# Reordering the chunk loop of a bidirectional state-space scan across four engines

## The reference, cut to what matters

```python
xbc = silu(depthwise_conv(xbc, w_ssm_conv[l], b_ssm_conv[l]))      # 7 taps
y_f = ssd_scan(xp, pad_front(dt_f), A[0], Bp, Cp)
y_b = fl(ssd_scan(fl(xp), fl(pad_front(dt_b)), A[1], fl(Bp), fl(Cp)))
y = (y_f + y_b)[:, PAD:] + d_skip.astype(f32)[:, None] * xf
# in ssd_scan, for each chunk of 128 tokens:
decay = exp(where(mask, seg, -inf)); cb = einsum('bclgn,bcsgn->bcgls', Cc, Bc)
y_diag = einsum('bcgls,bcgjls,bcsgjp->bclgjp', cb, decay, xd)
y_off = einsum('bclgn,bcgjpn,bcgjl->bclgjp', Cc, prev, exp(a_cs))
y = rms_norm(y * silu(z), w_ssm_norm[l]); branch_ssm = y @ w_ssm_out[l]
merged = sigmoid(gate_1) * branch_conf + sigmoid(gate_2) * branch_ssm
```

## Time and profile before

| | |
|---|---|
| device time, median of 3 runs | 2569.19 us (2568.33 to 2570.97) |
| the profiled execution, time | 2569.12 us |
| its span | 2567.1 us |
| busy: TensorE, weight load, VectorE, ScalarE, GpSimd | 95%, 60%, 63%, 32%, 16% |
| mean granted TensorE clock | 0.978 |
| DMA | 676.31 MB, mean 263 GB/s |
| chain that ended last, by engine | TensorE 69%, DMA 18%, VectorE 6%, ScalarE 4% |

### The profile page before, as it was taken

How to read it: one execution, slowest core, us unless ns; L and a number is a source line. 1 busy time by engine, 2 the same in 40 slices (tenths; PEclk the granted TensorE clock), 3 DMA queues, 4 the chain that set the end, 5 groups by cost and what they waited for, 6 DMA issues and landing times.

```text
span 2567.1 us, 41027 instructions
## 1 busy us (share of the span) xinstructions
PE 2439.5 (95%) x17615; PEld 1542.9 (60%) x17615; DVE 1610.1 (63%) x1749; ACT 821.3 (32%) x1361; POOL 406.9 (16%) x423
## 2 busy tenths in 40 slices
PE   8998899999989999999979989999999999999996
PEld 6764468888879898989879973333323233232232
DVE  4346556665539898988484641766666666666664
ACT  3256544444344645454454421000000000000001
POOL 0034011111102212123330400100000000011110
PEclk9999999999989999999989989999999999999998
DMA  5200268887745454546622467999999999999996
GB/s 201 84 33 25 94 236 288 291 285 270 269 151 187 153 188 152 193 147 210 175 100 104 182 249 304 376 411 413 411 412 412 412 412 414 413 413 411 411 413 235
DMA packets 129717, 676.31 MB, mean 263 GB/s; under 512 B 19300, under 2 KB 52068, under 8 KB 100228
## 3 DMA queue, kind: packets, MB, share of 16 engines
q1 hardware_dynamic: 56624, 554.81, 54.4%
q0 software_dynamic: 25632, 88.49, 10.2%
q10 hardware_dynamic: 47284, 30.42, 4.4%
HBM read 618.55 MB, written 55.12 MB: 262 GB/s over the span
## 4 chain that ended last, share of the span: by engine, by line
PE 69%; DMA 18%; DVE 6%; ACT 4%; issue 2%; POOL 1%; ACTq 0%; POOLq 0%; DVEq 0%
PE PS L1157 24%; DMA expert_ring_high<-w_experts 12%; PE PS L843 12%; PE PS L789 5%; PE PS L785 5%; PE PS L786 5%; PE PS L1025 4%; PE PS L1030 2%; DMA ring<-ssd_sums 2%; ACT ring L1566 2%; DMA projection_low_parts<-PREL 1%; PE PS L689 1%; PE PS L640 1%; PE PS L636 1%; PE PS L637 1%
## 5 line engine op out<-in xcount | busy, mean ns | idle before, releaser
L1157 PE MATMUL PS<-expert_ring_high,U 128*32 128x512 f32 x4240 | 472.4, 596 | 17.9 <-DMA expert_ring_high<-w_experts 17.2
L1157 PE MATMUL PS<-expert_ring_low,U 128*32 128x512 f32 x4016 | 446.9, 593 | 10.9 <-DMA expert_ring_low<-w_experts 9.3
L843 PE MATMUL PS<-XH,RINGF 128*128 128x264 f32 x2304 | 393.3, 289 | 1.2 <-ACT arena L1510 1.2
L1157 PEld LDWEIGHTS PS<-expert_ring_high,U 128*32 128x32 f32 x4240 | 136.5, 110 | 328.8 <-issue 303.0
L843 PEld LDWEIGHTS PS<-XH,RINGF 128*128 128x128 f32 x2304 | 325.3, 190 | 9.2 <-issue 6.8
L1157 PEld LDWEIGHTS PS<-expert_ring_low,U 128*32 128x32 f32 x4016 | 128.9, 110 | 309.1 <-issue 288.6
L2355 DVE SCALAR_TENSOR_TENSOR arena<-expert_ring_low,U,arena 128x2048 f32<-128x2048 f32 x134 | 305.7, 2347 | 0.0
L843 PE MATMUL PS<-UH,RINGF 128*128 128x264 f32 x1152 | 234.2, 286 | 0.0
L2088 DVE SCALAR_TENSOR_TENSOR H<-arena,par,H 128x528 f32<-128x528 f32 x240 | 187.5, 827 | 1.3
L843 PEld LDWEIGHTS PS<-UH,RINGF 128*128 128x128 f32 x1152 | 180.1, 190 | 0.0
L2355 DVE SCALAR_TENSOR_TENSOR arena<-expert_ring_high,U,arena 128x2048 f32<-128x2048 f32 x76 | 174.0, 2348 | 0.5
(11 more groups left out here) (358 smaller groups left out, 3886.3 us busy)
## 6 DMA issues: line engine op xcount, KB each, us to landing
expert_ring_low<-w_experts SPq DMA_DIRECT2D x96, 2048.0 KB, 27.7
expert_ring_high<-w_experts SPq DMA_DIRECT2D x96, 2048.0 KB, 30.3
arena<-w_proj POOLq DMA_DIRECT2D x72, 512.0 KB, 5.4
projection_low_parts<-PREL POOLq DMA_DIRECT2D x72, 512.0 KB, 4.2
ring<-w_proj SPq DMA_DIRECT2D x72, 512.0 KB, 3.6
RINGF<-projection_low_parts SPq DMA_DIRECT2D x72, 512.0 KB, 4.6
ring<-w_gu SPq DMA_DIRECT2D x11, 2048.0 KB, 10.4
ring<-ssd_sums ACTq DMA_DIRECT2D x32, 512.0 KB, 8.6
```

Source lines behind the costliest of these rows:

```text
L843: last = nc.tensor.matmul(PS[:, banks[i], 0:HT], w[:, k, :], x[:, k, lo:hi], start=start, stop=stop)
L1157: mm = nc.tensor.matmul(PS[QUAD * t:QUAD * t + QUAD, bank, :], stat(t), move(t), start=start, stop=stop)
```

## The change

It touches four lists. On GpSimd the masks move one step: the list is `XD(c)`, `XW(c)`, `masked(c + 1)` from chunk 1 on, where it was `masked(c + 2)` from chunk 0 on. On VectorE bank 6 is given back by the first read of `of`, ahead of the wait for `XD`, and the second `chunk_taps` moves behind that. On TensorE the last backward product of the last group comes between the two gate tiles of its first chunk. On ScalarE the exponentials of the last group's chunk 4 follow those of chunk 3. Behind the scan VectorE does `y_low(0)` and `y_low(1)`, the last `gate_y`, then `y_low` 2 to 7, two weight splits, `y_low` 8 to 15 and two weight splits; and GpSimd waits for four weight splits ahead of its last three `add_ln`.

```diff
--- before.py
+++ after.py
@@ -965,9 +965,15 @@
                     if c == 0:
                         open_(("cb", g, 0), 4)
                         fill(nc.tensor.matmul(PS[0:n, 4, 0:n], BF[:, 0:n], CF[:, 0:n], start=True, stop=True), ("cb", g, 0))
-                    gates((g, c))
-                    if c == 0:
+                    if c == 0 and g == GROUPS - 1:
+                        first, second = [GATE_OF[n] for n, place in enumerate(GATES_AT) if place == (g, 0)]
+                        proj(first)
                         back_state(g, 3)
+                        proj(second)
+                    else:
+                        gates((g, c))
+                        if c == 0:
+                            back_state(g, 3)
                     if c < 4 and g < GROUPS - 1:
                         conf(2 * g + CONF_AHEAD + c // 2, c % 2)
                     elif g < GROUPS - 1:
@@ -1645,8 +1651,10 @@
                 decays(g, 0)
                 decays(g, 1)
                 for c, (t0, n) in enumerate(CHUNKS):
-                    if c >= 2:
+                    if c >= 2 and not (g == GROUPS - 1 and c == NC - 1):
                         decays(g, c)
+                    if g == GROUPS - 1 and c == NC - 2:
+                        decays(g, c + 1)
                     if g == GROUPS - 1 and c + 2 < NC:
                         fr_load(g, c + 2)
                     gates_out((g, c))
@@ -2175,19 +2183,20 @@
 
                     if c > 0:
                         gate_y(g, c - 1)
-                    chunk_taps(g, c)
-                    dve.wait_ge(S("xd_ready"), i + 1)
                     yc = YC[0:n, :]
                     yh = yc.rearrange("p (h w) -> p h w", h=GH)
                     if c > 0:
                         got(dve, ("of", g, c))
-                        link(V_.tensor_tensor(yh, PS[0:n, 6, :].rearrange("p (h w) -> p h w", h=GH),
-                                              bc(EF[0:n, c, h8], n, HD), MUL))
-                        free(V_.tensor_tensor(yc, yc, XD[0:n, :], ADD), ("of", g, c))
+                        free(V_.tensor_tensor(yh, PS[0:n, 6, :].rearrange("p (h w) -> p h w", h=GH),
+                                              bc(EF[0:n, c, h8], n, HD), MUL), ("of", g, c))
                         dve.wait_ge(*freed(("of", g, c)))
+                        dve.wait_ge(S("xd_ready"), i + 1)
+                        link(V_.tensor_tensor(yc, yc, XD[0:n, :], ADD))
                         base = yc
                     else:
+                        dve.wait_ge(S("xd_ready"), i + 1)
                         base = XD[0:n, :]
+                    chunk_taps(g, c)
                     if c < 4:
                         got(dve, ("ob", g, c))
                         tmp = YB[0:n, :]
@@ -2213,18 +2222,17 @@
                             ins = V_.tensor_tensor(st, st, PS[:, 6, :], ADD)
                         free(ins, ("sf", g, c))
                         dve.wait_ge(*freed(("sf", g, c)))
-                    if g == GROUPS - 1 and c == NC - 1:
-                        for k in range(DT):
-                            y_low(k)
+            y_low(0)
+            y_low(1)
             gate_y(GROUPS - 1, NC - 1)
+            for k in range(2, DT):
+                y_low(k)
             tail_split_low(0)
             tail_split_low(1)
-            for k in range(8, 3 * QB):
+            for k in range(DT, 16):
                 y_low(k)
             tail_split_low(2)
             tail_split_low(3)
-            for k in range(3 * QB, 16):
-                y_low(k)
             conf_taps((tap[0] + DT * CONF_TAPS) // 2)
             tail_split_low(4)
             tail_split_low(5)
@@ -2560,8 +2568,8 @@
                         else:
                             got(pool, ("sb", g, 1))
                         scaled(XW[:, c % 2, :], g, c, n, W2[0:n, c, h8], "xwf_ready")
-                    if c + 2 < NC:
-                        masked(g, c + 2)
+                    if 1 <= c and c + 1 < NC:
+                        masked(g, c + 1)
                     if g == GROUPS - 1:
                         if c < 3:
                             add_ln(c + 1)
@@ -2570,6 +2578,7 @@
                                 add_y(k)
             for k in range(3 * QB, 16):
                 add_y(k)
+            pool.wait_ge(S("weights_low"), TAIL_LOW + 4)
             for u in range(4, DT - 1):
                 add_ln(u)
             pool.wait_ge(S("roots"), 4)
```

## The result

The changed kernel takes 2542.86 us (median of 5 runs, 2540.54 to 2545.98); the kernel before, run beside it, 2570.97 (2568.33 to 2572.76). The ratio is 0.9889, 95% interval 0.9878 to 0.9900: 28.1 us faster. The forecast was 2538.6 us, 30.5 less than before, with a range of 2530 to 2555.

What follows compares the result with a forecast made beforehand. TensorE was taken to bound the kernel, with its idle and slow time inside the scan winnable: 11.0 us in groups 0 to 2 plus 19.5 in the last group and first output tiles, 30.5 off 2569.12, gave 2538.6 us; range 2530 to 2555.

Steps and rivals of the forecast that it cites:

- Groups 0 to 2: First three scan groups: GpSimd's products fit inside the broadcast wait; idle 7.16 plus clock 5.1 us, 12.3 at most, 11.0 taken.
- First chunk: Last group: with the backward product between its two tiles, TensorE goes on without a wait, some 6 us earlier.
- Third chunk: Last group: with masks after the sums, its exponentials last from 1259 to 1264, below tiles until 1272.5; TensorE waits for nothing.
- Fifth chunk: Last group: exponentials follow the fourth chunk's, wait for GpSimd's mask until about 1282, end at 1285.5; chunk ends at 1295.4.
- Output tiles: Behind the last group: first tile ends at 1303.9, three more at 1321.4 against 1341.78; the 3.61 us wait goes.
- VectorE's gating comes third instead of ninth: Before the output tiles: squares and high parts of the last four rows start 17 us earlier.
- The added wait: GpSimd holds its last three convolution sums for four weight splits; VectorE gains, no engine misses the sums.
- Half: Rival: last group gives half, sums slow VectorE and one set of exponentials stays on the path; 2548.5 us, chance 0.13.
- nothing: Rival: the scan ends earlier but the tail waits for its weights or VectorE's taps; 2569 us, chance 0.05.
- A whole block: Rival: eight VectorE splits each held by a whole GpSimd sum of 1.66 us, losing 9.0 us more; 2544.6 us, chance 0.06.
- Slower: Rival: GpSimd's masks become late behind the products, 25 to 42 us if missed everywhere; 2584 us, chance 0.03.
- The signs I had named: Wrong if GpSimd's products wait for VectorE before a landed broadcast, or ScalarE waits over 3 us before fifth-chunk exponentials.

## Why the prediction was right

The waits it named are the ones that went, and 28.1 us came of 30.5. In two places luck helped, the clock of groups 0 to 2 and the first output tile. Step by step:

- **Groups 0 to 2: 11.0 forecast, 9.7 measured.** The products run inside the broadcast's wait, and VectorE never waits for exponentials there, so no mask is late where it counts (in group 0 3.64 and 1.36 us of cover are left; I had put some 3 before the fourth chunk's). The clock came back whole and gave 5.8 us, where I had 5.1 from rounded clocks: 0.7 us by luck. The term that was mis-sized is the short waits that stay: I left 1.3 us of the 12.3, and 3.31 us of the idle 7.16 stayed. Nearly all of it is L996 waiting 0.3 to 0.9 us for the output gate (3.3 us in G, before 0.4), because that gate, behind its pair of taps, has become what TensorE needs last. With that pair moved too, G fell by 2.0 us. I had also put VectorE's read of the second chunk at 865 before and 863 after; the rows have its end at 863.60 and 861.24. The step that "it need not wait here in later chunks either" held: L1002 waits nowhere for L2194.
- **Early return and mask order as two terms.** I gave them one sum, and rightly: undone alone they cost 5.3 and 11.3 us, together 9.0.
- **First chunk: 6 us forecast, 6.0 measured** with the backward product put back behind both tiles. It starts at 1222.46; I had put it near 1222.
- **Third chunk.** Its exponentials start 46.5 us into the group, forecast 1259 - 1212.3 = 46.7. The run with the old mask order confirms the chain that I named, mask, sum, square, exponentials.
- **Fifth chunk.** Its exponentials end at 75.2 us into the group; I had 73.2. They wait 1.97 us for GpSimd's fifth mask, which ends 71.9 us into the group where I had about 70. VectorE doesn't wait for these exponentials, but what stands behind them comes later by as much. That is a link that I hadn't written down: GpSimd's last `XD` product stands behind sums 9 to 11, which wait for squares that now stand behind these exponentials. The step was "fifth with 3.7 us of its own and three waits of some 0.9 us for VectorE": the three waits are 0.70, 0.29 and 3.09 us. And I had counted only VectorE's first split, not ScalarE's first weight tile, which comes last, by 0.97 us. The first output tile starts 85.3 us into the group; I had 1295.4 - 1212.3 = 83.1. These 2.2 us are nearly all of the 2.5 between the 20.4 that I worked out for L and the 17.9 measured; of the 2.5 I had allowed for 0.9 when I took 19.5.
- **Output tiles.** From the first matmul to the norm sum 26.1 us, forecast 1321.4 - 1295.4 = 26.0, and that is luck: I let the first tile wait for splits, while in fact it waits for none and runs most of its first 32 matmuls at half the clock, 6.83 us for 3.89, after TensorE's waits. The 3.61 us wait is gone, as said, and 2.50 us of it come back when the order is undone. "VectorE's gating comes third instead of ninth" gained nothing.
- **The added wait.** I called it harmless, and "VectorE gains" stands: 1.4 us of L. Beside sums a low part takes up to 1.6 to 1.8 us instead of 0.75, more than the 1217 ns average of the earlier trace rows, which was a mean of both kinds. I had also set that length against 689 ns from one start to the next; like against like, the eight lost 9.3 - 5.5 = 3.8 us and not 4.2. Four sums beside eight low parts cost 8.99 - 5.51 = 3.5 us, forecast some 3, and it is covered: no tile waits.
- **Rivals.** *Half* and *nothing* fell with L's 17.9 us and the unchanged rest. *A whole block* is nearer to what the traces show than I had allowed, only smaller. A sum takes 1.12 us where VectorE is idle (1281.80 in the changed kernel), not 1.66, and only four sums run beside the eight low parts, so the most that whole blocks could cost is 4 x 1.12 = 4.5 us, of which 3.5 were lost. It stayed under the tiles. The rule of the Trainium skill (SBUF — State Buffer, section "Who interferes with whom") is that the two engines' instructions shut each other out of a port that they share. The traces nearly agree: one low part and one sum take 1.57 us together, where a full block would make it 0.69 + 1.12 = 1.81. *Slower* was close in one place: the fourth chunk's mask in group 0 had 1.36 us to spare where I counted on some 3, and in group 1 nothing to speak of.
- **The signs I had named.** One sign of being wrong came up and cost nothing in G: in each of groups 0 to 2 GpSimd's products wait for VectorE with the landed broadcast of the fifth chunk behind them. In the last group the fifth mask, late behind sums and products, cost ScalarE 1.97 us. "No wait above 1 us before the output tiles" failed (3.09 us), the three groups gave 9.7 us instead of 10 to 12, and the first split came 12.7 us earlier in its group instead of 13 to 14. So the sign was badly chosen: a late mask counts only if an engine waits for it.

Undone one by one, the parts of the change give back in G and L 17.5 us (masks), 4.2 (bank), 7.9 (backward product, 1.9 of it the third group's clock), 8.2 (exponentials) and 4.5 (the order at the end with its wait), 42 in all, of the 27.6 that the change brought. They overlap: in the runs with the masks and with the exponentials undone, the wait that is opened again also pushes low parts into sums and lowers the clock behind it.

What stays open: why the rest scatters by 5 us between executions. No run aimed at it.

## What to carry to other kernels

An in-order queue with a DMA wait in it should have, ahead of that wait, all that doesn't need the transfer; the gain shows not at that queue but two or three engines further on (here GpSimd's queue, and TensorE's waits). A move is priced by following every instruction that it is put in front of, to who waits for that one: the two errors here, the taps ahead of a gate and the sums ahead of the last chunk's product, are both of that kind. And when a wait is taken out, look at what the earlier engine then runs beside: here 2.9 us gained became 2.9 us of slower VectorE.

## What the runs showed of the hardware that I had not expected

- A wait of TensorE can cost more than its length, and its length does not decide that. The same place in the third group, in the run with the order at the end undone and in the run with the backward product put back (whose L990 and L996 are the L996 and L1002 of the other):

```profile
1118.54 1.97 PE L996 MATMUL PS<-arena 128*128 128x64 f32 x16 [1.22 <-DVE arena L2078]
1120.35 1.08 PE L1002 MATMUL PS<-arena 128*128 128x512 f32 x2
```

```profile
1119.63 1.97 PE L990 MATMUL PS<-arena 128*128 128x64 f32 x16 [1.14 <-DVE arena L2072]
1121.43 1.96 PE L996 MATMUL PS<-arena 128*128 128x512 f32 x2
```

  After 1.22 us the clock stays at 2.4 GHz, while after 1.14 us it falls to 1.2 for what follows, and the group is 1.9 us longer, though both kernels run the same code there. In the changed kernel the wait there was 0.85 us, at full clock. With the masks put back, one of 1.98 us in group 0 was followed by an L1002 of 1.13 us, at full clock too. What decides is not shown. In G as a whole the clock was worth 5.8 of the 9.7 us.
- VectorE's low parts (two SBUF inputs) are slowed by GpSimd's sums to 1.57 us each (four in 6.27 us in the run with the old order at the end) from 0.69 without them, more than double; its weight splits likewise, two in 4.66 us against 2.35. The sums slow too, less: four take 6.19 us in the changed kernel, 1.55 each, against 1.12 for one where VectorE is idle.
